# Attention in a hybrid diffusion layer: two VectorE steps of the sample units given to GpSimd

## What is computed

```python
def row_block(i):                       # one grid row of queries
    bias = rpb32[:, row_bias_idx][:, :, col_bias_idx]
    s_loc = einsum('bnqhd,brnkhd->bhnqrk', q_row, k_blk) * ATTN_SCALE + bias
    s_loc = where(col_valid, s_loc, MASK_VALUE)      # -1e30 outside a window of 16 columns
    s_ctx = einsum('bnqhd,bphd->bhnqp', q_row, ctx_k) * ATTN_SCALE
    p = softmax(concatenate([s_loc, s_ctx], axis=-1), axis=-1)
    o = einsum(p_loc, v_blk) + einsum(p_ctx, ctx_v)
```

## Time and profile before

| | |
|---|---|
| median of 3 runs | 2456.88 us (2453.79 to 2462.15) |
| the profiled execution, by the timer | 2458.6 us |
| its span, first to last instruction | 2456.8 us |
| mean granted TensorE clock | 0.94 |
| busy: PE, PEld | 2213.2 us (90%), 1957.1 us (80%) |
| busy: DVE, ACT, POOL | 1146.5 us (47%), 760.4 us (31%), 94.7 us (4%) |

### The profile page before, as it was taken

One profiled execution on the slowest core, in us unless ns is written; L12 is line 12 of the kernel. 1 busy time (PEld: TensorE's weight loads), 2 busy tenths in 40 slices (PEclk: granted clock), 3 DMA queues, 4 the chain that ended last, 5 costly groups with the idle time before them and its releaser, 6 DMA issues.

```text
span 2456.8 us, 43926 instructions
## 1 busy us (share of the span) xinstructions
PE 2213.2 (90%) x19325; PEld 1957.1 (80%) x19325; DVE 1146.5 (47%) x2088; ACT 760.4 (31%) x1226; POOL 94.7 (4%) x140
## 2 busy tenths in 40 slices
PE   3789999999677888887987999999999999999996
PEld 2268888888555666667986999999999998887885
DVE  1222213554485778873336434444443443445444
ACT  2112222222353443432223333333332333333332
POOL 1000000000301111110000000000000000000000
PEclk8589999999876999998997999999999999999998
DMA  8977767776601000005323434334333344433341
GB/s 294 348 255 236 230 219 233 248 240 215 152 1 27 7 26 10 3 5 189 121 93 118 133 120 132 125 121 136 121 127 130 121 132 159 136 121 120 126 132 51
DMA packets 283038, 338.78 MB, mean 138 GB/s; under 512 B 9453, under 2 KB 268131, under 8 KB 280608
## 3 DMA queue, kind: packets, MB, share of 16 engines
q1 hardware_dynamic: 281008, 329.77, 41.9%
q0 software_dynamic: 1840, 6.20, 1.0%
HBM read 328.43 MB, written 10.28 MB: 138 GB/s over the span
## 4 chain that ended last, share of the span: by engine, by line
PE 79%; DVE 12%; DMA 5%; ACT 2%; issue 2%; POOL 0%; SPq 0%; DVEq 0%; POOLq 0%; ACTq 0%
PE ps L606 23%; PE ps L608 22%; PE ps L607 22%; DMA ring<-in_w_mod_dram 3%; PE ps L644 3%; PE ps L653 1%; PE ps L798 1%; PE ps L792 1%; PE ps L788 1%; DVE arena L1606 1%; DVE w_split L1311 1%; DVE u_buf L1687 1%; DMA arena<-in_x_sample_dram 1%; DVE stat L1467 1%; DMA ring<-in_w_out_dram 1%
## 5 line engine op out<-in xcount | busy, mean ns | idle before, releaser
L1311 DVE TENSOR_TENSOR w_split<-ring,w_split 128x1024 fp32r<-128x1024 f32 (+1 forms) x392 | 475.6, 1219 | 762.4 <-ACT w_split L1050 762.4
L1050 ACT ACTIVATE w_split<-ring 128x1024 fp32r<-128x1024 f32 (+1 forms) x392 | 406.6, 1050 | 729.3 <-PE ps L608 592.4
L606 PE MATMUL ps<-h_split,w_split 128*128 128x384 f32 x1776 | 599.6, 338 | 18.4 <-DVE w_split L1311 18.4
L608 PE MATMUL ps<-h_split,w_split 128*128 128x384 f32 x1776 | 596.5, 336 | 0.0
L607 PE MATMUL ps<-h_split,w_split 128*128 128x384 f32 x1776 | 596.4, 336 | 0.0
L606 PEld LDWEIGHTS ps<-h_split,w_split 128*128 128x128 f32 x1776 | 335.4, 189 | 30.0 <-issue 18.1
L607 PEld LDWEIGHTS ps<-h_split,w_split 128*128 128x128 f32 x1776 | 335.3, 189 | 0.0
L608 PEld LDWEIGHTS ps<-h_split,w_split 128*128 128x128 f32 x1776 | 335.2, 189 | 0.0
L606 PE MATMUL ps<-w_split,h_split 128*128 128x256 f32 x960 | 275.6, 287 | 9.3 <-DVE w_split L1311 9.3
L607 PE MATMUL ps<-w_split,h_split 128*128 128x256 f32 x960 | 272.6, 284 | 0.0
L608 PE MATMUL ps<-w_split,h_split 128*128 128x256 f32 x960 | 272.5, 284 | 0.0
(11 more groups left out here) (344 smaller groups left out, 2359.8 us busy)
## 6 DMA issues: line engine op xcount, KB each, us to landing
ring<-in_w_mod_dram SPq DMA_DIRECT2D x96, 1024.0 KB, 8.2
ring<-in_w_up_dram SPq DMA_DIRECT2D x88, 1024.0 KB, 5.1
ring<-in_w_in_dram SPq DMA_DIRECT2D x46, 1024.0 KB, 6.1
ring<-in_w_down_dram SPq DMA_DIRECT2D x44, 1024.0 KB, 5.4
ring<-in_w_out_dram SPq DMA_DIRECT2D x16, 1024.0 KB, 5.8
arena<-in_x_sample_dram SPq DMA_DIRECT2D x4, 1024.0 KB, 10.7
x_mid<-arena SPq DMA_DIRECT2D x1, 3072.0 KB, 10.2
h_f<-x_mid SPq DMA_DIRECT2D x1, 3072.0 KB, 12.8
```

Of the source, the lines that this page charges most:

```text
L606: mm(o_, lh, rh, start=start, stop=False)
L608: return mm(o_, ll, rh, start=False, stop=stop)
L1050: AC(wh[k % SPLITS][:, 0:width(n)], arrived(n), ACT.Copy).then_inc(s_hi, 1)
L1311: V.tensor_tensor(wl[k % SPLITS][:, 0:w], arrived(n), wh[k % SPLITS][:, 0:w].bitcast(F32), ALU.subtract).then_inc(s_lo, 1)
```

## The change

GpSimd waits for the bias table and adds the mask itself, and then makes the normalising multiply of units 12 to 35, each after a new semaphore `s_rc`. VectorE keeps the reciprocal of these units and no longer waits behind it. Before unit 12 VectorE waits for GpSimd's mask addition. The context units are as before.

```diff
@@ gpsimd, behind the tables of constants
             idb = idc.unsqueeze(1).broadcast_to([P, HH, CHUNK])
+            pool.wait_ge(s_Bm, 16 * 2 * HA)
+            pool_tt(Bm.rearrange("p h r c -> p (h r) c"), Bm.rearrange("p h r c -> p (h r) c"),
+                    consts[:, C_COL:C_COL + GRID].unsqueeze(1).broadcast_to([P, 6 * HA, GRID]), ALU.add).then_inc(s_Bmask, 1)
+            for u in range(HA, len(ATT)):
+                pool.wait_ge(s_rc, u - HA + 1)
+                nc.gpsimd.tensor_scalar(ss[:, u % 4, :], ss[:, u % 4, :], stat[:, 20 + u % 4:21 + u % 4], None, ALU.mult).then_inc(s_nr, 1)
             pool.wait_ge(s_pvc, len(ATT) // 2)
@@ vector, norm(u)
                 dv.wait_ge(s_ex, u + 1)
+                if t:
+                    V.reciprocal(stat[:, 20 + u % 4:21 + u % 4], stat[:, 16 + u % 4:17 + u % 4]).then_inc(s_rc, 1)
+                    return
                 link(V.reciprocal(stat[:, 20 + u % 4:21 + u % 4], stat[:, 16 + u % 4:17 + u % 4]))
@@ vector, the loop over the units
                 if u == HA:
-
-                    dv.wait_ge(s_Bm, 16 * 2 * HA)
-                    V.tensor_tensor(Bm.rearrange("p h r c -> p (h r) c"), Bm.rearrange("p h r c -> p (h r) c"),
-                                    consts[:, C_COL:C_COL + GRID].unsqueeze(1).broadcast_to([P, 6 * HA, GRID]), ALU.add).then_inc(s_Bmask, 1)
                     dv.wait_ge(s_Bmask, 1)
```

More of the change, by code:

```diff
@@ L362, in build @@
             "s_cbuf", "s_cmean", "s_ccen", "s_csq", "s_cvar", "s_cn", "s_cy"))
-        s_E0, s_E1, s_Bm, s_Bmask = sem("s_E0"), sem("s_E1"), sem("s_Bm"), sem("s_Bmask")
+        s_E0, s_E1, s_Bm, s_Bmask, s_rc = sem("s_E0"), sem("s_E1"), sem("s_Bm"), sem("s_Bmask"), sem("s_rc")
         s_cache, s_ckt, s_ckc, s_knt, s_knc, s_out = (sem(n) for n in (
```

## The result

Over five runs each the median is 2472.74 us against 2459.33 us before, a ratio of 1.0055 with a 95% interval of 1.0033 to 1.0077: 13 us, somewhere between 8 and 19. I had forecast 2459.5 us in 2450 to 2466, 2.6 us above the median of three runs known then. So the direction was right, and the size and the range were wrong. The profiled execution took 2469.25 us (span 2467.3), 10.65 us more than that of before. I use one measure throughout: the time from the reciprocal that ends the convolution's statistics to the first RWKV instruction on VectorE. It was 659.10 to 737.07, 77.97 us; in the changed kernel it is 657.53 to 746.07, 88.54 us. Those 10.57 us are as much as the two spans differ (10.5). That doesn't mean that the rest kept its length: the part ahead of the reciprocal was 1.57 us shorter, the part behind attention 1.5 us longer (1721.2 against 1719.7 us), and the two cancel.

A forecast was written before the change was run, and what follows sets the result against it. VectorE was taken to set the pace in attention's stretch from 700.0 to 731.2, TensorE at half clock before it. Terms 5.5 - 0.4 - 2.3 - 0.2 = +2.6 us from the median 2456.88 gave 2459.5 us, range 2450 to 2466.

The forecast's parts named there:

- parts 1 to 3: Up to the first sample unit: GpSimd's mask addition stalls L1450, softmax 9.7 us late, closed gap saves 4.2: 5.5 us late.
- part 4: Three sample pairs at half clock: TensorE is the bound, VectorE's shorter list saves nothing, fuller TensorE gives -0.4 us.
- part 5: Eight periods of sample pairs at full clock: from 3.48 to 3.2 us each, -2.3 us.
- part 6: Attention's tail, from the last pair's softmax: loses 0.45 us on VectorE, gains some 0.25 on GpSimd, -0.2 us.
- first rival: Mask addition: a long GpSimd instruction doesn't hold VectorE up; -7.1 us, 2449.8 us; chance 0.13.
- M: GpSimd's multiply of 384 columns in the sample pairs, taken as 0.6 us, bounds 0.5 and 1.0 us.
- The loop: Sample pairs: the odd unit's multiply on GpSimd, transpose, scores and next pair's first unit; period 2.56 + M, 3.2 us.
- third rival: Sample pairs: GpSimd paces the loop with M = 1.0, period 3.56; +5.5 us, 2462.4 us; chance 0.15.
- fixed part of the loop: Sample pairs: the period's terms besides GpSimd's multiply, 1.12 + 0.15 + 0.40 + 0.74 + 0.15 = 2.56 us.
- second rival: Mask addition: dearer on GpSimd, 15.1 instead of 9.8 us, so a longer stall; +7.9 us, 2464.8 us; chance 0.10.
- The fourth: Mask addition: the table lands after L1450, stalling the first prompt multiply some 7 us; about 0, 2457 us; chance 0.07.

The follow-up runs named there:

- e1: The change with the sample multiply taken back to VectorE, the mask addition staying on GpSimd; ratio 1.0020 against the kernel before, attention 81.98 us.
- e3: Against e1, GpSimd also waits for all eight L1450 subtractions before adding the mask; attention 81.69 us.
- e9: Kernel before with only the odd unit's multiply of each sample pair on GpSimd; pairs at full clock 4.10 us, attention 82.30 us.
- e8: Kernel before with only the even unit's multiply of each sample pair on GpSimd; pairs at full clock 3.48 us, attention 77.96 us.
- e6: Kernel before with the sample units' normalising multiply left out altogether; ratio 0.9988 against the kernel before, attention 75.05 us.
- e4: Against e1, the mask addition on GpSimd is cut into 24 instructions; attention 78.01 us.
- e5: Kernel before with 30 GpSimd instructions added in idle time, five forms at three widths; the multiply by a column took 1.24 us at 384 columns.

## Why the prediction was wrong

Step by step, measured from the start of L1450 (666.62 before, 665.06 after):

| step | forecast | measured |
|---|---|---|
| mask addition on GpSimd | 9.8 us | 9.89 us |
| parts 1 to 3: first sample unit | +5.5 us | +5.2 us (26.24 against 21.02) |
| part 4: first three pairs | -0.4 | +1.7 (14.12 against 12.38) |
| part 5: the eight periods | -2.3 | +4.9 (4.10 against 3.48) |
| part 6: the tail | -0.2 | -1.3 (7.82 against 9.16) |
| sum | +2.6 | +10.6 |

Parts 1 to 3 were right in the mechanism and nearly in the size: the first softmax came 9.0 us late instead of 9.7, and closing the gap brought 3.8 us instead of 4.2, since VectorE still stood idle for 1.1 us before the first sample unit. The hold seen over 0.9 us in the rows of RWKV did last for one of 9.9 us, and the first rival (no hold) falls with e1 and e3.

**Part 5 failed**, in the term M. The loop was the right one (e9, e8), but I priced GpSimd's multiply at 0.6 us because it reads one tensor, like the copy, with 1.0 us from the additions as the upper bound. It takes 1.23 to 1.25 us, above both ends: of the forms measured, this one and the multiply by a constant are the dearest. The third rival had M = 1.0 and named 1.2 us as the point from which the change would be clearly slower; the truth was just beyond it, so the range should have reached there. The fixed part of the loop was short too: 2.56 us forecast, 2.86 measured. I had counted 0.74 us for the first head's scores, where VectorE started only 0.95 us after their start, about when TensorE's timeline has both heads done (713.63; 712.68 to 713.60), although it waits for the first head alone; and 0.40 for transposes that take 0.48 when they begin from a wait. Against the forecast period of 3.2 us, M is worth 0.64 of the 0.9 us that each pair was longer, some 5 of the 7.2 us by which part 5 was off; the fixed part is the rest.

**Part 4** took the half-clock pairs as bound by TensorE and VectorE's savings as worthless there. With M in the loop TensorE was no longer the bound, and two of those pairs took 5.2 us; and e6, with no multiply at all, took 3.88 us for its second pair at the same half clock, against 4.30 before. **Part 6** missed that the tail stayed at full clock (1.00 in the third window); its 1.3 us covered some of part 4's miss, which was luck. The second rival (the addition at its dearer price) fell with 9.89 us: start-to-start spacing was the right way to read that price. The fourth didn't arise in the profiled execution: the table landed before L1450.

The profile's attention accounts for 10.6 us and the median of the runs for 13.4; the interval (8 to 19) holds both, and what a run adds beyond attention stays open.

## What to carry to other kernels

Price an instruction for another engine from the same operation on that engine: a copy and an addition there bound nothing, and a dozen lines in idle time measure it. Before giving work away, draw the loop it lies on: a step that an engine's full list makes look expensive may be worth 0.2 us a round, and on a slower engine it may be the whole period. A long GpSimd instruction stops some of VectorE's instructions to its end, so look for those beside it (here those with two inputs in SBUF, and the multiply from SBUF to SBUF), and move them, or cut it into pieces; then check in the trace that the pieces let VectorE in, since e4's did and the constant tables of e6 did not.

## What the runs showed of the hardware

- GpSimd multiplies 128 x 384 f32 by a column in 1.24 us, and in 0.83 us when the column is broadcast as a second tensor; a copy takes 0.50. The Trainium skill (GPSIMD Engine Reference, "Engine selection") has one-input work there at roughly line rate; the copy's 0.9 ns per column agrees, the multiply's 2.5 doesn't, and the measurement decides.
- A VectorE multiply from SBUF to SBUF of 128 columns stood 7.83 us behind a GpSimd addition, while reads of PSUM, a maximum and a reciprocal beside it kept their 0.28, 0.29 and 0.16 us.
- 24 GpSimd pieces of 0.59 us, each raising a semaphore, let eight VectorE instructions through in 5.42 us, one between two pieces. Four additions in a row for the tables of constants did not: a VectorE multiply of two SBUF inputs took 2.73 us instead of 0.57 and went on only about when the last of them ended (e6).
- The hold is mutual: a GpSimd multiply of 128 columns took 1.16 us instead of 0.45 behind a VectorE subtraction of 768 columns (e5).
